# Experts of a mixture on blocks of 128 tokens sorted by group, instead of on all 256 tokens

## The reference, cut to what matters

```python
def moe_ffn(h, router_w, router_b, w_gate, w_up, w_down):
    n = h.shape[0]                                    # 256 tokens, 1024 wide
    s = jax.nn.sigmoid((h @ router_w).astype(jnp.float32))          # 16 experts
    sel = (s + router_b).reshape(n, 4, 4)             # 4 groups of 4 experts
    top_v, top_i = lax.top_k(sel, 2)
    best = jnp.argmax(jnp.sum(top_v, axis=-1), axis=-1)             # one group per token
    loc = jnp.take_along_axis(top_i, best[:, None, None], axis=1)[:, 0]
    ids = best[:, None] * 4 + loc
    w = jnp.take_along_axis(s, ids, axis=1)
    w = w / jnp.sum(w, axis=-1, keepdims=True)
    combine = jnp.sum(jax.nn.one_hot(ids, 16) * w[..., None], axis=1)
    y = jnp.zeros(h.shape, jnp.float32)
    for e in range(16):
        a = jax.nn.silu(h @ w_gate[e]) * (h @ w_up[e])              # 1024 to 256
        y = y + combine[:, e:e + 1] * (a @ w_down[e])               # 256 to 1024
    return y
```

## Time and profile before

| | us |
|---|---|
| median of 3 runs | 2150.93 |
| lowest, highest run | 2150.33, 2153.35 |
| profiled execution | 2154.1 |
| its span, first to last instruction | 2152.8 |
| PE busy | 2031.5 (94%) |
| DVE busy | 1302.6 (61%) |
| ACT busy | 1009.7 (47%) |
| mean granted clock of TensorE | 0.975 |

### The profile page before, as it was taken

How to read it: one execution, slowest core, us unless ns; L and a number is a source line. 1 busy time by engine, 2 the same in 40 slices (tenths; PEclk the granted TensorE clock), 3 DMA queues, 4 the chain that set the end, 5 groups by cost and what they waited for, 6 DMA issues and landing times.

```text
span 2152.8 us, 29907 instructions
## 1 busy us (share of the span) xinstructions
PE 2031.5 (94%) x12765; PEld 1808.3 (84%) x12765; DVE 1302.6 (61%) x1582; ACT 1009.7 (47%) x1154; POOL 115.7 (5%) x54
## 2 busy tenths in 40 slices
PE   7799988999998999999998799999999999999998
PEld 2778877899997988899997699988789989888997
DVE  1647765455556656655679565565765566566554
ACT  2666663444444445533354543345543344455332
POOL 0480000002010000000000000000000000000000
PEclk9899999999999999999999899999999999999999
DMA  7771114365654444565541255553256555445552
GB/s 243 255 257 59 56 62 139 100 214 189 233 185 157 158 156 146 168 196 182 190 133 54 83 192 181 191 180 118 72 165 192 183 179 172 140 159 171 191 183 86
DMA packets 220510, 342.62 MB, mean 159 GB/s; under 512 B 6849, under 2 KB 171482, under 8 KB 220122
## 3 DMA queue, kind: packets, MB, share of 16 engines
q1 hardware_dynamic: 219826, 340.49, 48.0%
q10 hardware_dynamic: 552, 0.22, 0.0%
HBM read 339.64 MB, written 1.05 MB: 158 GB/s over the span
## 4 chain that ended last, share of the span: by engine, by line
PE 83%; DVE 8%; ACT 4%; DMA 2%; issue 1%; POOL 0%; SPq 0%; ACTq 0%; DVEq 0%; POOLq 0%
PE bank L529 14%; PE bank L530 14%; PE bank L531 14%; PE bank L512 11%; PE bank L513 11%; PE bank L514 11%; DVE wlo L1491 2%; PE bank L887 2%; ACT whi L1030 2%; DVE ARENA L2018 1%; DMA raw<-in_hg_w_in 1%; ACT ARENA L1041 1%; PE bank L591 1%; DMA ARENA<-in_ctx 1%; PE bank L672 1%
## 5 line engine op out<-in xcount | busy, mean ns | idle before, releaser
L1491 DVE TENSOR_TENSOR wlo<-raw,whi 128x2048 fp32r<-128x2048 f32 x292 | 683.1, 2341 | 431.1 <-ACT whi L1030 430.7
L529 PE MATMUL bank<-HH,whi 128*128 128x256 f32 (+1 forms) x2560 | 754.2, 295 | 19.8 <-DVE HL L1536 13.8
L530 PE MATMUL bank<-HL,whi 128*128 128x256 f32 (+1 forms) x2560 | 745.3, 291 | 0.0
L531 PE MATMUL bank<-HH,wlo 128*128 128x256 f32 (+1 forms) x2560 | 745.0, 291 | 0.0
L1030 ACT CAST whi<-raw 128x2048 fp32r<-128x2048 f32 x292 | 554.6, 1902 | 248.5 <-PE bank L514 221.0
L529 PEld LDWEIGHTS bank<-HH,whi 128*128 128x128 f32 x2560 | 498.2, 195 | 33.1 <-issue 18.5
L530 PEld LDWEIGHTS bank<-HL,whi 128*128 128x128 f32 x2560 | 498.7, 195 | 9.6 <-issue 1.9
L531 PEld LDWEIGHTS bank<-HH,wlo 128*128 128x128 f32 x2560 | 497.7, 194 | 5.3
L512 PE MATMUL bank<-whi,YH 128*128 128x512 f32 x864 | 340.9, 395 | 8.8 <-DVE YL L2062 5.6
L513 PE MATMUL bank<-wlo,YH 128*128 128x512 f32 x864 | 338.5, 392 | 0.0
L514 PE MATMUL bank<-whi,YL 128*128 128x512 f32 x864 | 337.5, 391 | 0.0
(11 more groups left out here) (289 smaller groups left out, 1743.5 us busy)
## 6 DMA issues: line engine op xcount, KB each, us to landing
raw<-in_ffn_w SPq DMA_DIRECT2D x128, 1024.0 KB, 5.4
raw<-in_ret_w_in SPq DMA_DIRECT2D x48, 1024.0 KB, 5.1
raw<-in_hg_w_in SPq DMA_DIRECT2D x20, 1024.0 KB, 5.7
ARENA<-in_w_mod SPq DMA_DIRECT2D x16, 1024.0 KB, 6.4
raw<-in_moe_w_gate SPq DMA_DIRECT2D x16, 1024.0 KB, 5.5
raw<-in_moe_w_up SPq DMA_DIRECT2D x16, 1024.0 KB, 5.3
raw<-in_moe_w_down SPq DMA_DIRECT2D x16, 1024.0 KB, 4.9
raw<-in_ret_w_out SPq DMA_DIRECT2D x16, 1024.0 KB, 4.9
```

The costliest lines, as they stand in the source:

```text
L529: pe.matmul(ps, w[0][:, k, c], ah, start=begin, stop=False, skip_group_check=True)
L530: pe.matmul(ps, w[0][:, k, c], al, start=False, stop=False, skip_group_check=True)
L531: x = pe.matmul(ps, w[1][:, k, c], ah, start=False, stop=k == 7, skip_group_check=True)
L1491: ve.tensor_tensor(wlo[n % NS][:, :], raw[i % NR][:, :], f32(whi[n % NS][:, :]), SUB).then_inc(*wlv("w", i))
```

## The change

Each token is put at a place in a list of five blocks of 128: the first 128 tokens of group g go to block g, and tokens of a group beyond 128 go to block 4 (two groups can't both have more than 128 of 256 tokens). TensorE counts the rank of each token in its group with a triangular matrix (`counts`), DVE makes the place matrices `PL` by comparing with a row of numbers, and TensorE gathers each block's scaled rows with them (`gathered`). Each of 20 units (block b, expert j of its group) computes gate and up with 128 tokens stationary and 256 weight columns streaming (`hidden`, 24 matmuls per item), then SiLU on ACT, one multiplication with the combine weight on DVE, two transposes (`turn`), high and low copies, and the down product into two banks (`down`, 12 matmuls). At the end of a block its output is split in two parts and scattered back to the tokens with the transposed place matrices (`scatter`), into the same four banks as before. The fifth block reads the weights of the overflowing group: SP reads the group number from `GI` into a register, and 12 loads take their address from it.

With that, the list has 60 MoE items, not 48. Two more raw buffers (in `ARENA`) are used from the eighth MoE item to the end of the stage. The routing comes before the first expert product, and it ranks both halves of the tokens in the same instructions. The last two chunks of the modulation are float32 matmuls on TensorE (`mod_late`, `mod_spread`); their four loads go out ahead of the third MoE item.

```diff
@@ weights
-    for e in range(17):
-        if e < 16:
-            plan(I["moe_w_gate"][0, e], 0, 8, 0, 256)
-            plan(I["moe_w_up"][0, e], 0, 8, 0, 256)
-        if e:
-            plan(I["moe_w_down"][0, e - 1], 0, 2, 0, 1024)
+    for n in range(21):
+        if n < 20:
+            expert("moe_w_gate", n, 8, 256)
+            expert("moe_w_up", n, 8, 256)
+        if n:
+            expert("moe_w_down", n - 1, 2, 1024)
@@ sync_program, load
+                if i == moe + 47:
+                    sp.wait_ge(*vec.at("chosen"))
+                    state["group"] = sp.value_load(GI[0:1, 0:1], min_val=0, max_val=3)
+                if moe + 47 <= i < moe + 60 and i != moe + 49:
+                    src = src(state["group"])
+                if held[i] is not None:
+                    sp.wait_ge(*(prj.at("item", held[i]) if held[i] in whole else wlow(held[i])))
+                elif place[i] >= NR:
+                    sp.wait_ge(*mm.at("mod_late", 11, 1))
@@ tensor_program, moe
+                def gathered(b, piece, bk):
+                    for k in range(4 * piece, 4 * piece + 4):
+                        for i in range(2):
+                            p = PL[i][:, 128 * b:128 * b + 128]
+                            x = pe.matmul(o, XN[i][:, c], p, start=i == 0, stop=i == 1)
...
+                def hidden(n, up):
+                    for k in range(8):
+                        x = mm3(bank[ps][:, 256 * up:256 * up + 256], hh[:, k, :], hl[:, k, :], w[0][:, k, :], w[1][:, k, :],
+                                k == 0, k == 7)
...
+                def down(n):
+                    for h in range(2):
+                        for k in range(2):
+                            x = mm3(bank[4 + h][:, :], ah[:, k, :], al[:, k, :], w[0][:, k, r], w[1][:, k, r],
+                                    j == 0 and k == 0, j == 3 and k == 1)
...
+                for n in range(21):
+                    b = n // 4
+                    if n < 20:
+                        hidden(n, 0)
+                    if n:
+                        turn(n - 1)
+                    if n < 20:
+                        hidden(n, 1)
+                    else:
+                        for y in range(4):
+                            scatter(y, 1)
+                    if n:
+                        down(n - 1)
+                    if n % 4 in (1, 2) and b < 4:
+                        gathered(b + 1, n % 4 - 1, 3)
+                    if n in (0, 3, 4):
+                        places((0, 3, 4).index(n))
+                    if n in (7, 8):
+                        mod_spread(n + 3)
+                    if n % 4 == 1 and n > 4:
+                        scatter(b - 1, 0)
+                scatter(4, 0)
+                scatter(4, 1)
@@ vector_program, moe, the loop
+                for n in range(21):
+                    if n % 4 == 1 and n > 4:
+                        outputs(b - 1, 0)
+                        outputs(b - 1, 1)
+                    if n % 4 in (2, 3) and b < 4:
+                        low(b + 1, n % 4 - 2)
+                    if 0 < n < 20:
                         take()
...
+                        ve.tensor_tensor(al, bank[bk][:, 0:256].rearrange("p (k n) -> p k n", k=2), f32(ah), SUB).then_inc(
+                            *vlo("moe_at", n - 1))
+                    if n < 20:
                         take()
+                        ve.scalar_tensor_tensor(AU[n % 2], AG[n % 2], CW[:, n:n + 1], bank[6 + n % 2][:, 256:512], MUL,
+                                                MUL).then_inc(*vps("moe_act", n))
+                    if n:
                         take()
```

More of the change, by code:

```diff
@@ L784, in moe @@
[L784 to L795 removed]
+                            k = 2 * q + m
@@ L1212, in moe @@
                 take()
                 ac.wait_ge(*mm.at("router"))
[L1214 removed]
+                ac.activation(sg, bank[2][:, 0:32], ACT.Sigmoid).then_inc(*aps("router"))
                 banks.free(("router",), aps)
[L1216 to L1221 removed]
```

522 lines of the change are left out of this document (358 added, 164 removed).

## The result

The changed kernel takes 2094.47 us (median of 4 runs, 2094.05 to 2095.53) where the kernel before took 2152.14 us on the same chip (4 runs, 2150.33 to 2154.25): a ratio of 0.9732, 95% interval 0.9716 to 0.9749, or 57.7 us less. The forecast was 2090 us, with 2070 to 2122 as its range.

A forecast was written before the change was run, and what follows sets the result against it. TensorE was taken to bound the MoE stage: start 29.6 + clock 5 + loop 205 + end 6.5 = 246 us against 307.1, 61 us less. Taken off the median of 2150.93 us, this gave 2090 us, range 2070 to 2122.

The forecast's parts named there:

- The loop: The 20 expert-and-block units of the MoE stage: 201 us of TensorE work plus 4 to 5 of stalls, 205 us.
- The stalls: Down matmuls in the loop wait for the activations' low part: 1 us per block, 4 to 5 us in all.
- The end: After the last down matmul: output copy, low part, scatter and four additions; last X 6.5 us after the loop.
- The start: Routing before the first expert matmul: 29.6 us after the mixer's last X, plus 5 us for low clock, partly in first unit.
- Twelve register loads: The fifth block's loads with an address from a register: taken as 0 us, bounds 0 and 66 us.
- The loads: 60 MoE loads of 1 MB instead of 48, issued five items ahead: hidden, costed at nothing.
- Rival 3, the clock: TensorE stays at 1.2 GHz through the loop, whose 201 us double: about 2290 us, slower than before; chance 0.04.
- The moved loads: Four w_mod loads move from the loop to the mixer's end, under its last matmuls (about 12 us of transfer): no cost.
- the prediction's own sign of being wrong: The whole would be wrong if the stage is not 240 to 250 us long, or stages outside it moved.
- The margin beneath TensorE: Loop, per unit: TensorE 10.05 us, DVE 8.4, ACT 7.6, so TensorE sets the loop.
- Rival 1: In-order queues stall TensorE before the down matmuls in every unit: 30 us more, about 2120 us; chance 0.10.
- Rival 2: Weight path paces the loop: 2107 us at 3.7 us per item, 2143 at 4.3; chance 0.11, 0.02 near 2143 or beyond.

The follow-up runs named there:

- x10_order: Changed kernel with the gathered half's modulation and copy behind ACT's first cast, its low part behind DVE's first weight low part: 2087.21 us, ratio 0.9695.
- x5_fixed: Changed kernel with the fifth block's 12 loads at a constant address (group 0), without the register load: 2092.86 us, ratio 0.9714.
- x4_raw3: Changed kernel with three raw buffers for the MoE stage instead of five: 2110.47 us, ratio 0.9800.
- x7_2of3: Changed kernel without the product of the activations' low part in gate and up (320 of 960 matmuls, 38 us of TensorE): 2091.68 us, ratio 0.9714.
- x1_loads: Changed kernel with the four late w_mod loads one item later, behind the third MoE item's load: 2088.71 us, ratio 0.9696.
- x13_2of3: x12_two without the product of the activations' low part in gate and up (320 of 960 matmuls): 2064.78 us, ratio 0.9578.
- x12_two: Changed kernel with the edits of x1_loads and x10_order together: 2086.47 us, ratio 0.9679.
- x9_wide: x1_loads with the 20 combine-weight matmuls at 128 columns instead of 4, with other numbers in them: 2090.75 us, ratio 0.9694.

## Why the prediction was right, point by point

**Right.** The stage: 246 us predicted, 245.0 measured.

- *The loop.* 205 us predicted, with 4 to 5 of it stalls; from the first expert matmul to the last down matmul (609.50 + 0.39 = 609.89) it is 206.7 us. Of these 1.7 are clock in the first units (0.13 and 0.21 of 5 us each), which leaves 205.0. The units, gathers, turns and scatters priced from the earlier trace rows were thus right to a microsecond. Gate loads go out 124.8 us apart for twelve units (430.47 and 555.27), 10.4 per unit; 10.2 was said. (The two gate loads of the earlier trace rows stand 16.99 us apart, not 16.98, which changes nothing.)
- *The stalls.* 4 to 5 us predicted from a layout, 3.8 measured in five waits; x10_order took them away and won 5.6. The layout had them behind a cast that starts 2 us late for ACT's own work. That ACT stands still until the gather is done (20.2 us in eight waits) was not in it.
- *The end.* 6.5 us predicted, 609.89 to 616.54 = 6.7 measured.
- *The start.* 29.6 us plus a part of the 5 for the clock; 31.6 measured. The part of the ranking for which the counts wait ended (388.23) 14.9 us before the first expert matmul, 14.7 were said. Ahead of it the chain took 16.7 us rather than 14.9: the transposes had been priced at the lower clock, the router had not (6.84 us). If the 2.0 us beyond 29.6 are all the clock's, it cost 3.7 us together with the 1.7 in the first units, of the 5 set aside for it.
- *Twelve register loads.* Nothing, as taken (x5_fixed).
- *The loads.* Nothing, as taken: no cast waited in the loop. The reason was the five buffers, and x4_raw3 shows what they cover: 13 us.
- *Rival 3, the clock.* 0.99 in the loop. The rule of the Trainium skill, "TensorE: Matmul & The Clock Gate", section "HAM oscillation — how this bites in real kernels", by which bursts with waits between them fall back to the low clock each time, did not decide here: the waits in the loop are 0.8 us at the longest, and no stretch of 5 us behind 410 was below 1.00. Where there were longer waits the traces agree with it: at the start, with gaps of 3 to 6 us, and in the loop of x7_2of3, where the clock fell at four of sixteen waits. The 0.04 of this rival thus rested on the waits being short.

**Wrong, and what stands in its place.**

- *The moved loads.* "Four `w_mod` loads inside the loop, which move to the end of the mixer, where about 12 us of transfer lie under its last matmuls", was costed at nothing. This is the step that failed: they hold up the item queued behind them (15.5 us of landing), whose cast and low part stand in front of the mixer's last additions on ACT and DVE. Price: 2.8 us (x1_loads). Room for the bytes was there; what was asked for in that room was not looked at. By the prediction's own sign of being wrong, a stage outside the MoE moved, and one of its 60 loads landed after 15.5 us where below 10 was said. The other 2.1 us by which X came later are the shift between executions, already there at the first MoE load (326.50 against 324.45).
- *The margin beneath TensorE.* DVE was said to be at 84% and ACT at 76% of a unit, and the loop to belong to TensorE by that distance. DVE is at 78%, yet x7_2of3 shows that the loop, with its queues in this order, could be only 2.8 us shorter. The stalls of a unit were counted one by one as small costs. They were the visible end of a chain (gather on TensorE, modulation and high copy of the gathered half on ACT, the casts behind them, their low parts, the low part of the activations) that was about as long as TensorE's own. The forecast did not suffer by it, since TensorE still had the most work, but the margin was about 3 us. Rival 1 was near it: it also has in-order queues that stall TensorE before the down matmuls, at 20 × 1.5 us. With 38 us less of matmuls there are 16 such waits of 1.8 us; the changed kernel had five.

Rival 2 with 3.7 us per item is refuted: in x13_2of3, from the first expert matmul (403.78) to the end of the last down matmul (579.93 + 0.39), an item took 176.5 / 60 = 2.94 us.

The total: 61 us predicted, 57.7 measured between the medians and 58.6 between the profiled executions. In the latter the stage gave 1 us more than said; the mixer's end took back 2.8, the shift between executions 2.1, and the rest of the program gave 1.5. The shift is chance; where the 1.5 us lay stays open.

## What to carry to other kernels

Busy shares tell which engine sets the end, not by how much: in-order queues on two engines that are three quarters busy can be as long a chain as the full one, and the way to see it is to take work off the full one and look what waits. Look above all for an operation that waits for the full engine itself with work for later units queued behind it, as the modulation of a gathered half here. A load that is moved costs what is queued behind it, so look up what the next item's cast and low part stand in front of before a full queue is called free. And when work is moved into an idle gap, compare its length with the gap: what fits keeps the clock up, what doesn't delays the chain.

## What the runs showed of the hardware

- TensorE's granted clock at the start of the stage went by the idle time ahead of it: the lower level behind 5.7 us or more, the full one behind none, and either behind 3.08 us, with the same code. In the loop of x7_2of3 it fell to 0.66 to 0.76 (over 5 us) at four of 16 waits, the shortest of them 1.75 us, and not at three others of 2.67 us; in x13_2of3, with waits of up to 1.5 us, it stayed at 1.00. The 48 short matmul records of transposes and router took 10.5 us in the changed kernel and 5.8 in x1_loads.
- The clock also fell while TensorE was busy, without a gap, at places that changed from kernel to kernel (0.66 from 400 to 405 in x10_order, 1.00 there in x12_two, whose start has the same matmuls). What decides this stays open; whether the width of the matmuls does, x9_wide could not show.
- 16 DMA engines kept up 356 and 362 GB/s over stretches of 30 us, with 1 MB items, in x13_2of3; the full stretch of the earlier trace rows had 333. Landing times rise before the DMA engines are full: a median of 5.5 us for the gate loads before (205 GB/s in the loop), 6.5 to 6.9 for the three rows of the changed kernel (296 GB/s), and 15.5 for the item behind four other loads.
